# First layer's token shift joined with the rwkv operands, and the rotary table made inside the first mixing projection

## What is computed

```
prev = jnp.pad(p_shift, ((0, 0), (1, 0), (0, 0)))[:, :-1]
xs = p_shift + (prev - p_shift) * mu_shift
r, k, v, wd, ad = jnp.split(xs, SHIFT_SPLITS, axis=-1)
wlog = -jax.nn.softplus(-(w0 + jnp.tanh(wd) @ w_up)) - 0.5
a = jax.nn.sigmoid((a0 + ad @ a_up).astype(f32))
kk = k * k_k
kk = kk / jnp.maximum(jnp.sqrt(jnp.sum(kk * kk, axis=-1, keepdims=True)), 1e-12)
k = k * (1.0 + (a - 1.0) * k_a)
...
inv = ROPE_THETA ** (-jnp.arange(0, QK_ROPE, 2, dtype=F32) / QK_ROPE)
ang = positions.astype(F32)[..., None] * inv
return jnp.cos(ang), jnp.sin(ang)
```

## Time and profile before

| what | us |
|---|---|
| median of 3 runs | 5985.95 |
| lowest, highest | 5983.98, 5993.72 |
| the profiled execution | 5987.98 |
| its span in the trace | 5986.2 |
| busy: TensorE, VectorE, ScalarE, GpSimd | 5247.4, 2806.5, 2156.0, 365.9 |

### The profile page before, as it was taken

The page is one execution under the profiler, slowest core; times in us unless marked ns, Lnnn a source line. Parts: engine busy times, 40 slices in busy tenths (PEclk is TensorE's granted clock), DMA queues, the critical chain, the costliest instruction groups (busy, mean ns, idle before and its releaser), DMA issues. The chain is left out here.

```text
span 5986.2 us, 96973 instructions
## 1 busy us (share of the span) xinstructions
PE 5247.4 (88%) x38308; PEld 4573.7 (76%) x38309; DVE 2806.5 (47%) x4371; ACT 2156.0 (36%) x3202; POOL 365.9 (6%) x573
## 2 busy tenths in 40 slices
PE   6973775986999969999798996999999999999994
PEld 5662774765777759999687775989898999999994
DVE  2596332533184445555416533444444555555444
ACT  2212111632244334444323442333333444444432
POOL 0112000000050000000003200100000000000001
PEclk8995997997999979999899997999999999999997
DMA  2110001012100165555210143444444455555544
GB/s 75 43 57 2 2 2 77 1 60 98 39 4 18 68 257 210 193 197 207 106 42 15 46 137 138 164 151 163 163 148 163 179 187 188 194 186 190 185 158 177
DMA packets 110042, 701.50 MB, mean 117 GB/s; under 512 B 12608, under 2 KB 16464, under 8 KB 68432
## 3 DMA queue, kind: packets, MB, share of 16 engines
q1 hardware_dynamic: 95888, 651.28, 30.1%
q0 software_dynamic: 9088, 28.48, 1.3%
q10 hardware_dynamic: 4800, 17.83, 0.7%
HBM read 633.16 MB, written 64.38 MB: 117 GB/s over the span
## 5 line engine op out<-in xcount | busy, mean ns | idle before, releaser
L3179 DVE TENSOR_TENSOR experts_low<-experts_raw,experts_high 128x1024 fp32r<-128x1024 f32 x678 | 810.8, 1224 | 1005.1 <-ACT experts_high L3108 1005.1
L3043 PE MATMUL ps<-experts_xs_high,experts_high 128*128 128x256 f32 (+1 forms) x3584 | 1038.0, 290 | 35.9 <-issue 34.4
L3043 PE MATMUL ps<-experts_xs_low,experts_high 128*128 128x256 f32 (+1 forms) x3584 | 1040.9, 290 | 0.0
L3043 PE MATMUL ps<-experts_xs_high,experts_low 128*128 128x256 f32 (+1 forms) x3584 | 1039.6, 290 | 0.0
L3043 PEld LDWEIGHTS ps<-experts_xs_high,experts_high 128*128 128x128 f32 x3584 | 681.9, 190 | 48.5 <-issue 39.1
L3108 ACT ACTIVATE experts_high<-experts_raw 128x1024 fp32r<-128x1024 f32 x678 | 687.5, 1048 | 35.2 <-DMA experts_raw<-experts 35.2
L3043 PEld LDWEIGHTS ps<-experts_xs_low,experts_high 128*128 128x128 f32 x3584 | 680.0, 190 | 9.5
L3043 PEld LDWEIGHTS ps<-experts_xs_high,experts_low 128*128 128x128 f32 x3584 | 681.0, 190 | 0.0
L2718 PE MATMUL ps<-dense_xs_parts,dense_high 128*128 128x256 f32 x2816 | 498.7, 280 | 4.0 <-DVE dense_xs_parts L2821 2.7
L2718 PEld LDWEIGHTS ps<-dense_xs_parts,dense_high 128*128 128x128 f32 x2816 | 436.3, 189 | 12.3 <-issue 4.8
L3035 PE MATMUL ps<-experts_high,experts_hid_high 128*128 128x512 f32 x1120 | 444.6, 397 | 0.0
(11 more groups left out here) (538 smaller groups left out, 9142.3 us busy)
## 6 DMA issues: line engine op xcount, KB each, us to landing
experts_raw<-experts SPq DMA_DIRECT2D x226, 1536.0 KB, 6.4
dense_raw<-dense SPq DMA_DIRECT2D x90, 1536.0 KB, 6.3
mixT<-w_in SPq DMA_DIRECT2D x36, 512.0 KB, 3.3
y_slot<-mla_blank SPq DMA_DIRECT2D x15, 1152.0 KB, 20.5
out_proj_raw<-w_out SPq DMA_DIRECT2D x48, 256.0 KB, 2.7
proj_keys_raw<-w_in SPq DMA_DIRECT2D x20, 512.0 KB, 3.2
x_mixed<-x_out SPq DMA_DIRECT2D x16, 512.0 KB, 4.7
y_slot<-experts_y ACTq DMA_DIRECT2D x8, 1024.0 KB, 8.3
```

What stands on the lines that cost most here:

```text
L3043: last = nc.tensor.matmul(ps[:, m, 0:width], w[:, u, m, c], x[:, k, 0:width], start=(k == 0 and i == 0), stop=(k == KD - 1 and i == 2))
L3179: nc.vector.tensor_tensor(low[:, v, t, :], raw[:, v % NR, t, :], high[:, v, t, :].bitcast(F32), ALU.subtract).then_inc(split, 1)
```

## The change

The stage `shift_tokens` is gone, and its work is done inside `rwkv_operands`. GpSimd subtracts for nine blocks (`small`, k, v) into two tiles of `bonus`, which is not in use yet; VectorE subtracts for the four r blocks itself. The first token is updated by VectorE in one column with `less`, which is minus `mu`. The `small` block comes first (after r's block 0), then k and r in turn, with the key scalings between them, and v between the scans. The squares on ScalarE stand between its first and its last four gates. GpSimd takes over cum less rate and a times kk. Easing, keys and r_k products come ahead of the division by the length, whose spread copies go through `bonus` rather than `tmp`. The kk-times-exponent products come ahead of those of r, and ScalarE's exponents in the same order.

`rope_tables` is gone as a stage. In the first mixing layer `projections_and_norms` gets `table`; SP loads the positions behind the first two weight blocks, VectorE reduces the angles behind the first two splits, ScalarE does the Sin behind the sixth block ahead of the squares, and VectorE negates ahead of the sums of squares.

```diff
-            shift_tokens(core, big, small)
...
 def rwkv_operands(core, big, small, decay_end, bonus, rate, cum):
+    blocks = [(12, small[:, :])] + [(4 + j, K[:, j, :]) for j in range(4)] + [(8 + j, V[:, j, :]) for j in range(4)]
+    diff, own = bonus[:, 0:2, :], bonus[:, 2:4, :]
...
+        def _(pool):
+            for n, (_, p) in enumerate(blocks):
+                if n >= 2:
+                    pool.wait_ge(step, 2 * (n - 1))
+                nc.gpsimd.tensor_tensor(diff[:, n % 2, 1:T], p[:, 0:T - 1], p[:, 1:T], ALU.subtract).then_inc(subtracted, 1)
+            pool.wait_ge(scanned, 4)
+            for j in range(4):
+                nc.gpsimd.tensor_tensor(rate[:, j, :], cum[:, j, :], rate[:, j, :], ALU.subtract).then_inc(before, 1)
+            pool.wait_ge(gates, 8)
+            pool.wait_ge(eased, 4)
+            for j in range(4):
+                pool.wait_ge(unit, j + 1)
+                nc.gpsimd.tensor_tensor(A[:, j, :], A[:, j, :], KK[:, j, :], ALU.mult).then_inc(removed, 1)
...
+            act.wait_ge(step, 2)
             nc.scalar.activation(low[0:32, :], small[0:32, :], ACT.Tanh).then_inc(lowr, 1)
...
+            def shift(n):
+                m, p = blocks[n]
+                dve.wait_ge(subtracted, n + 1)
+                stt(p[:, 0:1], p[:, 0:1], less[:, m:m + 1], p[:, 0:1], ALU.mult, ALU.add).then_inc(step, 1)
+                stt(p[:, 1:T], diff[:, n % 2, 1:T], core.v("mu", m), p[:, 1:T], ALU.mult, ALU.add).then_inc(step, 1)
+            def shift_own(j):
+                p = R[:, j, :]
+                tt(own[:, j % 2, 1:T], p[:, 0:T - 1], p[:, 1:T], ALU.subtract).then_inc(own_diff, 1)
+                dve.wait_ge(own_diff, j + 1)
+                stt(p[:, 0:1], p[:, 0:1], less[:, j:j + 1], p[:, 0:1], ALU.mult, ALU.add).then_inc(own_step, 1)
+                stt(p[:, 1:T], own[:, j % 2, 1:T], core.v("mu", j), p[:, 1:T], ALU.mult, ALU.add).then_inc(own_step, 1)
...
+            shift_own(0)
+            shift(0)
+            for j in range(4):
+                shift(1 + j)
+                if j:
+                    shift_own(j)
+                key(j)
             dve.wait_ge(gates, 4)
...
                 nc.vector.tensor_tensor_scan(cum[:, j, :], core.c("restart"), rate[:, j, :], 0.0,
                                              ALU.mult, ALU.add).then_inc(scanned, 1)
+                shift(5 + j)
...
-            rope_tables(core, table)
...
 def projections_and_norms(core, name, weights, xT, segments, down, room, z, gains, table=None):
+            if table is not None:
+                sp.dma_start(room[:, 2, :].bitcast(I32), core.dram["positions"].to_broadcast([P, T])).then_inc(angles, 16)
...
             def behind(s):
+                if s == 0 and table is not None:
+                    act.wait_ge(reduced, 1)
+                    nc.scalar.activation(table, table, ACT.Sin).then_inc(sines, 1)
...
+            for n in range(2):
+                split_block(n, n)
+            if table is not None:
+                reduce_angles()
+            pairs(dve, first, lambda n, u, i: split_block(n, u), first=2)
+            if table is not None:
+                dve.wait_ge(sines, 1)
+                nc.vector.tensor_scalar(table[64:96, :], table[64:96, :], -1.0, None, ALU.mult)
```

More of the change, by code:

```diff
@@ L428, in projections @@
     st.end()
[L431 to L461, removed]
 def rwkv_operands(core, big, small, decay_end, bonus, rate, cum):
@@ L474, in rwkv_operands @@
     one_ka = st.sb("one_ka", [P, 4])
+    less = st.sb("less", [P, 13])
     length = st.sb("length", [P, 3, 8 * NT])
@@ L489, in _, with gate @@
             sp.wait_ge(loaded, 32)
+        @block.gpsimd
+        def _(pool):
[11 more added lines that the diff above has]
+                nc.gpsimd.tensor_tensor(A[:, j, :], A[:, j, :], KK[:, j, :], ALU.mult).then_inc(removed, 1)
         @block.scalar
         def _(act):
+            def gate(n):
+                m, j = divmod(n, 4)
+                act.wait_ge(lora, n + 1)
+                nc.scalar.activation((rate if m == 0 else A)[:, j, :], two(j), ACT.Sigmoid,
+                                     bias=core.v("w0" if m == 0 else "a0", j)).then_inc(gates, 1)
+            act.wait_ge(step, 2)
             nc.scalar.activation(low[0:32, :], small[0:32, :], ACT.Tanh).then_inc(lowr, 1)
             nc.scalar.activation(low[32:64, :], small[32:64, :], ACT.Copy).then_inc(lowr, 1)
[L495 to L502, removed]
+            for n in range(4):
+                gate(n)
             for j in range(4):
@@ L506, in _ @@
                 nc.scalar.activation(tmp[:, j, :], KK[:, j, :], ACT.Square).then_inc(squared, 1)
+            for n in range(4, 8):
+                gate(n)
             act.wait_ge(lengths, 1)
@@ L515, in _ @@
             for j in range(4):
+                act.wait_ge(before, j + 1)
+                nc.scalar.activation(rate[:, j, :], rate[:, j, :], ACT.Exp).then_inc(e2, 1)
+            for j in range(4):
                 act.wait_ge(heads, j + 1)
                 nc.scalar.activation(tmp[:, j, :], cum[:, j, :], ACT.Exp).then_inc(e1, 1)
-            for j in range(4):
-                act.wait_ge(before, j + 1)
-                nc.scalar.activation(rate[:, j, :], rate[:, j, :], ACT.Exp).then_inc(e2, 1)
             for j in range(4):
@@ new lines, in _ @@
+            for j in steps:
+                ts(tmp[:, j, :], A[:, j, :], core.v("k_a", j), one_ka[:, j:j + 1], ALU.mult, ALU.add).then_inc(eased, 1)
+            for j in steps:
+                dve.wait_ge(eased, j + 1)
+                dve.wait_ge(keyed, j + 1)
+                tt(K[:, j, :], K[:, j, :], tmp[:, j, :], ALU.mult).then_inc(keys, 1)
+            dve.wait_ge(own_step, 8)
+            for j in steps:
+                dve.wait_ge(keys, j + 1)
+                stt(tmp[:, j, :], R[:, j, :], core.v("r_k", j), K[:, j, :], ALU.mult, ALU.mult).then_inc(products, 1)
@@ L589, in _ @@
[L589 to L598, removed]
+                tt(KK[:, j, :], KK[:, j, :], two(j), ALU.mult).then_inc(unit, 1)
@@ L599, in _ @@
+            dve.wait_ge(step, 2 * len(blocks))
             for j in steps:
                 dve.wait_ge(heads, j + 1)
-                nc.vector.tensor_tensor(bonus[:, j, :], two(j), V[:, j, :], ALU.mult)
-            dve.wait_ge(removed, 4)
+                tt(bonus[:, j, :], two(j), V[:, j, :], ALU.mult)
+            for j in steps:
+                dve.wait_ge(e2, j + 1)
+                dve.wait_ge(unit, j + 1)
+                dve.wait_ge(removed, j + 1)
+                tt(KK[:, j, :], KK[:, j, :], rate[:, j, :], ALU.mult)
```

99 lines of the change are left out of this document (39 added, 60 removed).

## The result

The changed kernel takes 5928.75 us (median of 4 runs, 5924.01 to 5936.44), the kernel before on the same chip 5986.32 (4 runs, 5983.98 to 5993.72). The ratio is 0.9904, with a 95% interval of 0.9892 to 0.9916. 5932.6 was forecast, with a range of 5921 to 5945. The profiled execution took 5936.44 with a span of 5932.8; against the span before, 5986.2, that is -53.4, the forecast sum. It is the slowest of the four, though: the medians are 57.6 apart.

What follows compares the result with a forecast made beforehand. TensorE is busiest overall, but in the removed stretch VectorE and GpSimd take turns and barriers make stage time kernel time. -37.3 (merged stage) and -16.1 (rotary table) give -53.4, from median 5985.95 to 5932.6 us; range 5921 to 5945.

Steps and rivals of the forecast that it cites:

- The merged stage, -37.3: Token shift and operands in one stage: 102.6 us against 139.9 before, so 37.3 us off.
- GpSimd's turns, 23.3: Merged stage: time VectorE sits out GpSimd's operations, 1.4 for the first and 12 x 1.82 = 21.8, together 23.3 us.
- Margin of 1.3 at the root: Merged stage: root there at 52.5, VectorE through scans and shifts at 53.8, so it loses nothing, by 1.3 us.
- VectorE's own work, 76.6: Merged stage: VectorE's operations, from shift updates to the last eight products, sum to 76.6 us.
- Case D: Rival, merged stage: length chain binds, small block late, root after 53.8; 3 us late gives 5934; no chance given.
- a times kk at no cost beside divisions: Merged stage: GpSimd's last 4 operations, beside VectorE products with one PSUM input, booked at nothing; if uncovered, 7.3 us.
- case B: Rival, merged stage: turns cost more, beside PSUM-input products too (5940) or 2.87 each (5948); chance 0.13.
- Scalings locked (8.3 us of them): Merged stage: VectorE's scalings, 8.3 us, also take turns with GpSimd; if free, the stage is some 6.3 us shorter.
- case A: Rival, merged stage: turns cost less, 5926 with only the scalings free, 5923 with no turns; chance 0.15.
- The rotary table, -16.1: Rotary stage removed: -15.7 for the stage, +0.9 for a TensorE stop, -1.3 for the norm's root table load.
- spare time of 1.32: First mixing projection: eighth block's split ends at 1491.51, TensorE needs it at 1492.83; Sin's 2.24 leaves a 0.9 us stop.
- Case C: Rival, first mixing projection: the stop drops TensorE's clock, 10.9 us per block at 1.2 GHz, up to 6052; chance 0.01.

Runs made afterwards that it cites:

- the fifth experiment: The changed kernel plus four GpSimd subtractions whose results nobody uses, beside VectorE's last eight products in the merged stage; 5940.45 us, one execution.

## Why the prediction was right

**The merged stage, -37.3: right, 102.3 measured for 102.6.** Its terms were less exact than their sum.
- *GpSimd's turns, 23.3.* They came to 19.9. The nine shift turns cost 14.2, added up as each record's excess over its own time: 1.90 and 1.81 for scalings of 0.18 and 0.17, the key scaling 1.5, one-column updates 1.5 to 1.6 each. The prediction had 16.0 for them: it took 1.82 per turn where 1.5 to 1.7 is what the next VectorE operation is held up. Cum less rate cost 5.7 in records (2.32 less 0.19, 6.52 less 2.97) for 7.3; the rest of those four, 2.34 each, lay mostly in the wait for the root. The experiment without any such turn gives the same from the other side: 102.3 - 95.6 = 6.7 gained, after adding nine subtractions at 1.26 and four at 1.14 to VectorE (15.9) and losing the root's 2.2, makes 20.4.
- *Margin of 1.3 at the root.* This step failed in sign: shifts through at 50.8 in place of 53.8, root at 53.0 in place of 52.5, and so a wait of 2.2 in place of none. The prediction had ten turns in front of the last shift update, 17.8 in all; there were nine, since GpSimd's first cum less rate began only behind that update, and they cost 14.2. So VectorE came early and the chain through the lengths did bind. Case D had that effect by another road (small block late, root after 53.8), and neither came true: the small block was done at 7.8 for 7.4, the root at 53.0. The errors of the three terms, -3.4, +2.2 and +1.0 (next point), nearly cancel, which is luck.
- *VectorE's own work, 76.6.* What is left of 102.3 less 19.9, 2.2 and the bonus waits is 77.6. About 0.4 of the difference is in the 13 one-column updates, behind which the next operation starts 0.13 later for the 0.10 assumed.
- *Waits for head sums, 2.7.* Measured 0.97 + 0.68 + 0.49 + 0.49 = 2.6.
- *a times kk at no cost beside divisions.* Right: 4.60 for four divisions; case B falls.
- *Scalings locked (8.3 us of them).* Right, against case A: key scaling 2.26 for 0.74, easing 6.52 for 2.97. This was the choice that no row of before decided. By the Trainium skill, SBUF — State Buffer, section Who interferes with whom, such scalings can take the port pair that VectorE shares with GpSimd, for a whole instruction. The trace agrees; what the fifth experiment adds is that VectorE kept GpSimd out over a row of eight instructions.

**The rotary table, -16.1: right but for the stop.** The lead is 38.1 where the rotary stage began (1360.37 less 1322.28), 53.8 at the norm and 55.1 at the projection, so the stage gave 15.7 and the root's table load 1.3, as forecast. The 38.1 are 0.8 more than the merged stage's 37.3; they came in between, in code that did not change. The stop was 1.17 for 0.9. The delay behind it was as forecast: from the table load at 1428.04 to the first square it is 2.26 us, and the eighth block's split starts 10.56 behind the copy in front of the squares (1437.55 less 1426.99) for 8.32 before (1490.28 less 1481.96), 2.24 later. Mis-sized was the spare time of 1.32: TensorE ran out of work at 1438.92 - 1.17 = 1437.75, which leaves 1.2, and it started 0.15 after the split's end (1437.55 + 1.22 = 1438.77). The Sin starts as the load ends (1428.04 + 1.28 = 1429.32, Sin at 1429.33). The Trainium skill, ScalarE: Activation LUTs, section What ACT_TABLE_LOAD costs, adds a drain of about 1.38 us to a switch; it does not show here either. That the stop would count in the sum was wrong: the projection takes 214.41 for 214.37, because the clock is low for 3.4 us less.

**Case C (clock) fell.** 1.00 on both sides of the stop. **The sum** of -53.4 stood to the tenth in the span, partly by luck: the lead was 54.9 in front of the experts (3724.41 less 3669.49), and the expert loads, 3.2 longer in this execution, took some of it back.

## What to carry to other kernels

An elementwise GpSimd operation beside VectorE operations that read two SBUF tiles, or scale, is not parallel work: a shift subtraction cost VectorE 1.5 to 1.7 us where doing it itself costs 1.2, so give GpSimd only what lies beside PSUM reads or waits. Two short stages on the same data are worth merging when one leaves TensorE idle: here the low-rank products and gates came to lie beneath the shift. A gain read off one stage shows in that stage's records long before it shows in the times, when a later part varies by 10 us from run to run. Several terms that err both ways can still add up to the right sum: compare term by term with the records before trusting the model.

## What the runs showed of the hardware

- VectorE operations of 13 and 4 columns (0.18 and 0.17 alone) took 1.90 and 1.81 beside a GpSimd subtraction, and a scaling of 1024 columns 2.26 for 0.74: a turn cost 1.5 to 1.7 whatever the width.
- Four divisions that read PSUM took 4.60 with GpSimd's four products across them (9.32): no turn.
- Eight VectorE products without a pause kept GpSimd out for 8.7 us; in another place GpSimd came in between two updates that had no pause either (3.44 for 1.28).
- A GpSimd subtraction takes 1.89 with both inputs in one block and 2.34 with inputs in two.
- At 32 products of one column, with TensorE booked as busy all the time, the granted clock fell from 1.00 to 0.50 in all ten executions, 2.5 to 4.9 us after the start of the first of them, and stayed there for 3.4 or 6.8 us.
